# The sine product of q in rotary attention: from TensorE and VectorE to GpSimd

## What is computed

```python
def apply_rope(x, cos, sin):
    # rotate-half rotary on the last axis, x [B,T,H,2,64]
    x1, x2 = jnp.split(xf, 2, -1)
    return jnp.concatenate([x1 * cos - x2 * sin, x2 * cos + x1 * sin], -1)

def diff_attention(x, cos, sin, w_in, ...):
    q, k, v = jnp.split(x @ w_in, 3, axis=-1)
    q = apply_rope(q, cos, sin)
    k = apply_rope(k, cos, sin)
    lam = exp(sum(lam_q1 * lam_k1)) - exp(sum(lam_q2 * lam_k2)) + lambda_init
    ...
    s = einsum('bqhcd,bkhcd->bhcqk', q_blk, k) * scale     # causal
    p = softmax(s)
    p = p[:, :, 0] - lam * p[:, :, 1]
    o = einsum('bhqk,bkhe->bqhe', p, v)
    ...
    return (rms_norm(o, subln_w) * (1.0 - lambda_init)) @ w_out
```

## Time and profile before

| | us |
|---|---|
| median of 3 runs | 1422.12 |
| lowest and highest run | 1420.06, 1423.38 |
| the profiled execution, its own time | 1420.63 |
| span of that execution, first to last instruction | 1418.9 |

### The profile page before, as it was taken

One profiled execution on the slowest core, in us unless ns is written; L12 is line 12 of the kernel. 1 busy time (PEld: TensorE's weight loads), 2 busy tenths in 40 slices (PEclk: granted clock), 3 DMA queues, 4 the chain that ended last, 5 costly groups with the idle time before them and its releaser, 6 DMA issues.

```text
span 1418.9 us, 20021 instructions
## 1 busy us (share of the span) xinstructions
PE 1383.6 (98%) x7038; PEld 1135.0 (80%) x7038; DVE 869.4 (61%) x1362; ACT 635.3 (45%) x1033; POOL 80.8 (6%) x91
## 2 busy tenths in 40 slices
PE   8799999999999999999999999999999999999997
PEld 7688888888788888888888776667788888888886
DVE  4576677777586666666425537777686666664226
ACT  5666556666224444443212235666424444443211
POOL 3000000000000000000002011111000000000002
PEclk9999999999999999999999999999999999999999
DMA  6222111211222333334332222121223333334231
GB/s 195 55 65 68 45 51 52 63 55 60 75 60 67 100 100 89 103 96 152 105 104 74 89 60 60 45 74 59 90 60 89 89 103 92 100 118 134 89 104 60
DMA packets 157728, 118.85 MB, mean 84 GB/s; under 512 B 5899, under 2 KB 145645, under 8 KB 157677
## 3 DMA queue, kind: packets, MB, share of 16 engines
q1 hardware_dynamic: 157676, 118.17, 27.7%
HBM read 116.04 MB, written 2.11 MB: 83 GB/s over the span
## 4 chain that ended last, share of the span: by engine, by line
PE 90%; DVE 5%; ACT 3%; DMA 1%; issue 1%; SPq 0%; DVEq 0%; ACTq 0%
PE bank L1666 13%; PE bank L1668 13%; PE bank L1667 13%; PE bank L1681 10%; PE bank L1654 8%; PE bank L1655 8%; PE bank L1656 8%; PE bank L1735 3%; PE bank L2062 1%; PE bank L1742 1%; PE bank L2080 1%; PE bank L1733 1%; PE bank L2023 1%; PE bank L1751 1%; PE bank L1632 1%
## 5 line engine op out<-in xcount | busy, mean ns | idle before, releaser
L368 DVE TENSOR_TENSOR w_lo<-raw,w_hi 128x1024 fp32r<-128x1024 f32 x194 | 237.7, 1227 | 241.9 <-ACT w_hi L363 236.6
L1666 PE MATMUL bank<-x_hi,w_hi 128*128 128x512 f32 (+1 forms) x912 | 348.6, 382 | 2.6 <-DVE x_lo L1042 2.0
L1668 PE MATMUL bank<-x_hi,w_lo 128*128 128x512 f32 (+1 forms) x912 | 340.5, 373 | 0.0
L1667 PE MATMUL bank<-x_lo,w_hi 128*128 128x512 f32 (+1 forms) x912 | 340.2, 373 | 0.0
L363 ACT ACTIVATE w_hi<-raw 128x1024 fp32r<-128x1024 f32 x186 | 195.1, 1051 | 166.6 <-PE bank L1656 139.5
L1666 PEld LDWEIGHTS bank<-x_hi,w_hi 128*128 128x128 f32 x912 | 172.2, 189 | 33.8 <-DVE x_lo L1042 2.4
L1667 PEld LDWEIGHTS bank<-x_lo,w_hi 128*128 128x128 f32 x912 | 172.3, 189 | 30.2 <-issue 1.9
L1668 PEld LDWEIGHTS bank<-x_hi,w_lo 128*128 128x128 f32 x912 | 172.0, 189 | 30.4
L1654 PE MATMUL bank<-w_hi,u_hi 128*128 128x512 f32 x416 | 164.2, 395 | 0.6 <-DVE w_lo L368 0.6
L1656 PE MATMUL bank<-w_hi,u_lo 128*128 128x512 f32 x416 | 162.0, 389 | 0.0
L1655 PE MATMUL bank<-w_lo,u_hi 128*128 128x512 f32 x416 | 161.9, 389 | 0.0
(11 more groups left out here) (294 smaller groups left out, 2000.2 us busy)
## 6 DMA issues: line engine op xcount, KB each, us to landing
raw<-in_ffn_w_up SPq DMA_DIRECT2D x88, 512.0 KB, 3.8
raw<-in_ffn_w_down SPq DMA_DIRECT2D x44, 512.0 KB, 3.3
raw<-in_gdn_w_in SPq DMA_DIRECT2D x32, 512.0 KB, 4.1
raw<-in_diff_w_in SPq DMA_DIRECT2D x24, 512.0 KB, 3.8
raw<-in_gdn_w_out SPq DMA_DIRECT2D x8, 512.0 KB, 3.3
raw<-in_diff_w_out SPq DMA_DIRECT2D x8, 512.0 KB, 3.3
x_tok<-in_x SPq DMA_DIRECT2D x4, 512.0 KB, 5.9
ROW<-decay_rows SPq DMA_DIRECT2D x8, 256.0 KB, 4.6
```

The lines of the kernel that those rows point to most:

```text
L368: nc.vector.tensor_tensor(w_lo[:, s, :], raw[:, (base + r) % RAW, :], w_hi[:, s, :].bitcast(F32), ALU.subtract).then_inc(lo_ready, 1)
L1666: nc.tensor.matmul(out, hi, x_hi[:, k, cols], start=(k == 0), stop=False)
L1667: nc.tensor.matmul(out, hi, x_lo[:, k, cols], start=False, stop=False)
L1668: ins = nc.tensor.matmul(out, lo, x_hi[:, k, cols], start=False, stop=last)
```

## The change

The sine product of q no longer uses PE. After `rope_cos` of q, POOL makes `rope2` of q in four operations of 32 partitions: the inputs are 32 partitions of `qk_raw` and of `sin`, the output is the neighbouring 32 partitions of `rope2`, so the exchange of the halves is made by the output's place. POOL waits for each before the next. The sign is not in the product: DVE computes once, while the FFN of the layer before runs, a column of plus and minus ones from `swap` (`signs`), and its sum for `qr` becomes one operation, `rope2 * sign + rope1`. k keeps its matrix product. In the program of DVE the step of q moves behind `att_o`.

```diff
@@ -603,16 +604,27 @@
                 nc.gpsimd.tensor_tensor(rope1[kind][:, :], qk_raw[kind][:, :], cos[:, :],
                                         ALU.mult).then_inc(rope_pool, 1)

+            def rope_sin(g):
+
+                pool.wait_ge(rope_pool, 2 * g + 1)
+                for b in range(4):
+                    src, dst = slice(32 * (b ^ 1), 32 * (b ^ 1) + 32), slice(32 * b, 32 * b + 32)
+                    nc.gpsimd.tensor_tensor(rope2[0][dst, :], qk_raw[0][src, :], sin[src, :],
+                                            ALU.mult).then_inc(q_sin, 1)
+                    pool.wait_ge(q_sin, 4 * g + b + 1)
+
             def take_v(g):

                 nc.gpsimd.tensor_copy(vh[:, :, :], v_tok[:, :, ds(g * P, P)]).then_inc(v_head, 1)

             rope_cos(0, 0)
+            rope_sin(0)
             rope_cos(0, 1)
             take_v(0)
             with pool.Fori(0, HEADS - 1) as h:
-                for kind in range(2):
-                    rope_cos(h + 1, kind)
+                rope_cos(h + 1, 0)
+                rope_sin(h + 1)
+                rope_cos(h + 1, 1)
                 pool.wait_ge(t_pe, 1 + TP_N * h + TP["pv"])
                 take_v(h + 1)
             affine(3)
...
@@ -948,7 +960,7 @@

                 act.wait_ge(chunk_done, C_QK + 2 * g + kind + 1)
                 if not (isinstance(g, int) and g == 0):
-                    act.wait_ge(rope_pool, 2 * g + kind - 1)
+                    act.wait_ge(*((q_sin, 4 * g) if kind == 0 else (rope_pool, 2 * g)))
                 nc.scalar.activation(qk_raw[kind][:, :], bank[kind][:, :], ACT.Copy,
                                      scale=(HD ** -0.5 if kind == 0 else 1.0)).then_inc(bank_read[kind], 1)

...
@@ -1426,6 +1438,10 @@
                 dve.wait_ge(lam_dve, 1)
                 nc.vector.tensor_reduce(small[:, 0:2], lamp[:, :, :], AX.X, ALU.add).then_inc(lam_dve, 1)

+            def signs():
+
+                nc.vector.tensor_reduce(small[:, 7:8], swap[:, :], AX.X, ALU.add, negate=True).then_inc(sign_ready, 1)
+
             def lambda_rest():
                 dve.wait_ge(lam_act, 1)
                 nc.vector.tensor_tensor(small[:, 6:7], small[:, 3:4], small[:, 2:3], ALU.subtract).then_inc(lam_dve, 1)
...
@@ -1507,16 +1524,21 @@
             split_lo(dve, C_QK, 0, 2)
             dve.wait_ge(rope_act, 2)
             dve.wait_ge(lam_dve, LAM_DVE)
+            dve.wait_ge(sign_ready, 1)

             def rope(g, kind):
                 name = "qk"[kind]
                 last = R_DVE0 + RD_N * g
-                dve.wait_ge(rot_pe, 2 * g + kind + 1)
-                nc.vector.tensor_tensor(rope2[kind][:, :], bank[4 + kind][:, :], sin[:, :], ALU.mult).then_inc(rope_head, 1)
-                dve.wait_ge(rope_head, last + RD["rope2 " + name])
-                dve.wait_ge(rope_pool, 2 * g + kind + 1)
-                dst = (qr, kr)[kind]
-                nc.vector.tensor_tensor(dst[:, :], rope1[kind][:, :], rope2[kind][:, :], ALU.add).then_inc(rope_head, 1)
+                if kind == 0:
+                    dve.wait_ge(q_sin, 4 * g + 4)
+                    nc.vector.scalar_tensor_tensor(qr[:, :], rope2[0][:, :], small[:, 7:8], rope1[0][:, :], ALU.mult,
+                                                   ALU.add).then_inc(rope_head, 1)
+                else:
+                    dve.wait_ge(rot_pe, g + 1)
+                    nc.vector.tensor_tensor(rope2[1][:, :], bank[5][:, :], sin[:, :], ALU.mult).then_inc(rope_head, 1)
+                    dve.wait_ge(rope_head, last + RD["rope2 k"])
+                    dve.wait_ge(rope_pool, 2 * g + 2)
+                    nc.vector.tensor_tensor(kr[:, :], rope1[1][:, :], rope2[1][:, :], ALU.add).then_inc(rope_head, 1)

             def n_own(h, name):
                 dve.wait_ge(n_dve, ND_N * h + ND[name])
...
@@ -1594,12 +1616,13 @@
                 mix(3)
                 if more:
                     split_lo(dve, C_QK, it, 2 * r + 5)
-                    rope(h + 1, 0)
                 else:
                     hold_lo(dve, C_ATT_OUT + 5)
                 dve.wait_ge(t_pe, 1 + h * TP_N + TP["pv"])
                 nc.vector.tensor_scalar(att_o[:, :], bank[3][:, :], ROOT_MAX, -ROOT_MAX, ALU.min,
                                         ALU.max).then_inc(n_dve, 1)
+                if more:
+                    rope(h + 1, 0)
                 if not more:
                     hold_lo(dve, C_ATT_OUT + 6)
                 dve.wait_ge(n_act, NA_N * h + NA["sq"])
...
@@ -2017,10 +2040,10 @@
                         pe.wait_ge(bank_read[kind], T_QK // 2 + g + 1)
                     block_products(kind, (C_QK + 2 * odd + kind) % WS, k, k == KT - 1)

-            def rotate(g, kind):
-
-                wait_read(pe, kind, T_QK // 2 + g)
-                nc.tensor.matmul(bank[4 + kind][:, :], swap[:, :], qk_raw[kind][:, :], start=True,
+            def rotate_k(g):
+
+                wait_read(pe, 1, T_QK // 2 + g)
+                nc.tensor.matmul(bank[5][:, :], swap[:, :], qk_raw[1][:, :], start=True,
                                  stop=True).then_inc(rot_pe, 1)

             def turned_out(h):
...
@@ -2107,8 +2130,6 @@
                 turn(2)
                 fill(11, 13)
                 values(2)
-                if not last:
-                    rotate(h + 1, 0)
                 turn(3)
                 fill(13, 15)
                 values(3)
...
@@ -2118,7 +2139,6 @@
             pe.wait_ge(v_out, 2)
             project_qk(0, 0, 0, 2 * KT)
             pe.wait_ge(v_out, 2 * NT)
-            rotate(0, 0)
             step(0, 0)
             with pe.Fori(0, PAIRS - 1) as it:
                 for r in (1, 2):
```

More of the change, by code:

```diff
@@ L315, in build @@
         t_pe, t_dve, t_act, v_head = sem("t_pe"), sem("t_dve"), sem("t_act"), sem("v_head")
+        q_sin, sign_ready = sem("q_sin"), sem("sign_ready")
         rot_pe, rope_pool, rope_head = sem("rot_pe"), sem("rope_pool"), sem("rope_head")
@@ L1449, in down @@
                         lambda_rest()
+                        signs()
                 if l == 0:
@@ L2086, in step @@
                 fill(0, 1)
-                rotate(h, 1)
+                rotate_k(h)
                 fill(1, 3)
@@ L2158 @@
                      ("turn", 1), ("sc", 3, 0), ("sc", 3, 1), ("turn", 2), ("turn", 3), "pv"])
-RD, RD_N = numbered(["rope2 q", "qr", "rope2 k", "kr"])
+RD, RD_N = numbered(["qr", "rope2 k", "kr"])
 ND, ND_N = numbered(["oc", "ms", "inv", "flag", "o", "lo"])
```

## The result

| | before | with the change |
|---|---|---|
| median, us | 1421.24 (6 runs) | 1426.18 (6 runs) |
| lowest and highest, us | 1420.06, 1423.38 | 1425.38, 1428.22 |
| profiled execution, its own time and span, us | 1420.63, 1418.9 | 1425.85, 1424.1 |
| mean granted clock | 0.995 | 0.993 |

The ratio is 1.0037 with a 95% interval of 1.0024 to 1.0050: the change makes the kernel some 5 us slower, which is more than 0.2%. First the page of the changed kernel: busy time by engine, then the shares of the chain that ended last.

The account below looks back on a forecast made before the run. The tensor engine (PE), busy 98% of the span with 90% of the chain, was taken as the bound. 1.9 - 0.1 + 6 x 0.35 = +3.9 us on a median of 1422.12 gave 1426.0 us, range 1416 to 1432.

Parts of the forecast that it names:

- the sum of the change: Whole kernel: 1.9 us lost at the start, 0.1 gained to head 1, six steady heads 0.35 longer each: +3.9 us.
- Duration of a pass: Each GpSimd product of 32 partitions by 512 takes 1.27 us, since time goes by elements of a partition.
- The exclusion: GpSimd operations and VectorE operations with two SBUF inputs shut each other out for their whole length.
- some 0.13 us: In a collision, the held operation ends its own time less some 0.13 us after the one holding it.
- The walk through a steady head: Step-by-step times for head 3: held passes delay qr and kr, scores start at 929.95 instead of 929.62, 0.35 us longer.
- The start: Before head 0 nothing covers the passes; first scores at 845.0 instead of 843.08, 1.9 us lost.
- Then qr to 841.35: At the start, qr follows the last pass (840.61) and ends at 841.35, before POOL's cosine of k ends at 842.50.
- my third rival: Steady heads: GpSimd's cosine of k beats qr at 926.9; 0.9 us more in six heads, about 1431; chance 0.12.
- Head 0 to head 1: In this step pass 4 ends ahead of the reduction, 0.76 of 0.86 us is lost at Pm: gains 0.1 us.
- the rival of the clock: Longer PE waits at heads' ends bring the clock down in two to six heads: 3 to 9 us more; chance 0.12.
- The saving arrives: Pass 4 ends by 925.4, each of seven heads gives 0.86 us, distance 20.4: -6.0 us, about 1416; chance 0.20.
- half of it: Passes near 1.1 us or fewer collisions: heads within 0.3 us of today, start +1, 1420 to 1424; chance 0.12.

Follow-up runs that it names:

- the start repaired: The changed kernel, but q of head 0 made as before with swap product and VectorE product, passes only from head 1: 1423.68 us, ratio 1.0015.
- two passes: The changed kernel with two GpSimd passes of 64 partitions instead of four of 32, the exchange of the halves left out: 1417.04 us, ratio 0.9973.
- the last experiment: The changed kernel with GpSimd's four passes waiting until Pm of the head's fourth block is written: 1440.97 us, ratio 1.0136.

## Why the prediction was right, and where it was off

**The time.** Forecast 1426.0 us, measured 1426.18; range and direction hold. Two small errors cancel in that closeness: the sum of the change was +3.9 us where the medians differ by 4.9, and I started from a median of 1422.12 that six runs put at 1421.24. The mechanism and the sign were worked out; that the figure is only 0.2 us off is luck.

**Duration of a pass: 1.27 us, independent of the partitions.** Right: 1.26 to 1.30 alone for 32 partitions, 1.29 for the one free pass of 64, and 1.26 to 1.30 for the free cosine products of 128. The Trainium skill, GPSIMD Engine Reference, section 3.1, gives about 2.6 cycles an element, an estimate of 1.11 us; the trace disagrees by 0.16 us, and the measurement decides. By the page's figure a head would have been about 0.4 us shorter, about even with the kernel before, and the sign of the result less clear.

**The exclusion.** Right, and shown three ways: passes that nobody reads cost 3.6 us, the same DVE operation takes 1.66 us with its second input in SBUF and 0.68 with it in PSUM, and a single-input copy on POOL held kr. That is the rule of the Trainium skill, SBUF, State Buffer, section Who interferes with whom, and every row here agrees with it. The scaling of Eb (one input), which I let hold pass 1 by that rule, did: pass 1 took 1.42 us, not 1.27. One size was off: the "some 0.13 us" that a held operation gains fits passes, w_lo and kr, but a held Pm of 0.62 us ended 0.41 after its holder by the prediction's own rows, 0.21 less, and the fourth Pm of the changed kernel 0.19 less. It is worth 0.07 us.

**The walk through a steady head.** Shift it by 3.97 us, the later end of the cosine product, and compare: pass 1 ends 925.51 by the walk and 925.50 in the trace, Pm 926.13 and 926.06, pass 2 927.28 and 927.20, w_lo 928.36 and 928.28, pass 3 929.51 and 929.41, pass 4 930.85 and 930.78, kr 933.87 and 933.81, the scores 933.92 and 933.86. The net of +0.35 us a head (929.95 - 929.62 is 0.33) was measured as 0.30. What is late next was kr, as said, and two of its parts were tested alone: the copy of v is worth 0.25 us, and the swap product put back costs nothing.

**The start: +1.9 forecast, +2.4 measured.** The passes ended where they should (840.86 by the walk shifted by 0.25 us, 840.92 in the trace). The step that failed is "Then qr to 841.35": POOL's cosine product of k won the race by 0.05 us and held qr to 842.80. This is the mechanism of my third rival, which I had placed in the steady heads and not here. w_lo then was held by the copy of v. Together 0.5 us.

**Head 0 to head 1: -0.1 forecast, +0.7 measured.** The step that failed is the rival of the clock: I asked whether new waits inside the heads bring the clock down, and not whether the longer wait that I forecast at the start makes the old drop last longer. It did, 6.8 us at half clock instead of 3.4, and with the start repaired the step is 1.2 us shorter. Without it the passes gain 0.48 us there, more than the 0.1 that I walked: the walk kept the cosine product ahead of the third Pm, as in the earlier trace rows, and in the trace the race fell the other way, so that PE's wait of 0.96 us for that Pm is gone.

**The other rivals.** The clock did not fall within the heads of the change after waits of 1.35 us; that it falls after 2.4 us, at 1.55 us a time, one experiment shows. The change sat 1 us of wait a head away from a loss four times as large. The saving arrives when the passes are off POOL: 20.44 us a head, the very figure that I had named for it, and with two passes half of it.

## What to carry to other kernels

Before work is moved to an idle GpSimd, count its operations, not its elements, and look at what VectorE does beside them: each operation with two SBUF inputs there is shut out for a whole GpSimd operation. A VectorE operand left in PSUM avoided the conflict here. An operation of 32 partitions cost as much as one of 128, and the cost of a chain of them is not linear: here two fitted into a cushion of half a microsecond ahead of a late chain, and four did not.

When a saving lies on a busy engine, ask first whether that engine waits further on in the same period; here PE's product, put back, filled waits and cost nothing. And a wait that grows has a second price, the granted clock behind it, that can exceed the wait itself: 1.55 against 0.7 us a head in the last experiment.

## What the runs showed of the hardware that I had not expected

- Races between the two engines are decided by 0.03 to 0.13 us, and identical code falls differently in two places of one run: at the start POOL led by 0.05 us, in the steady heads DVE by 0.12.
- The clock after a wait of PE, in the profiled executions: no drop after 0.56, 1.35, 1.42, 1.74 and 1.79 us, a drop of some 3.4 us after 2.12, 2.15 and 3.56 us, of 6.8 to 6.9 us after 4.54, 5.12, 5.13 and 5.14. Between 2.3 and 2.5 us both occur: 2.31 and 2.38 without, 2.40 to 2.48 with. A drop of 3.4 us costs 1.0 to 1.6 us.
- The clock is not the same in all executions of one kernel: of the ten of the kernel with VectorE passes from SBUF, four have a mean clock of 0.996 and take 1415.9 to 1417.4 us, three have 0.994 and take 1418.8 to 1419.1. Differences of 2 us between medians can be the clock's.
- A single input in SBUF on VectorE is enough to hold a GpSimd pass (Eb, 1.42 against 1.27 us) and to be held by one (with the passes alone, Eb of the fourth block in head 0 takes 1.32 instead of 0.55 us). The reduction of the squares kept its 0.68 to 0.69 us beside GpSimd in all kernels, and the operations that read PSUM (the product of k, att_o) neither held GpSimd nor were held.
- Operations of 32 partitions whose output lies on other partitions than their inputs take the time of ordinary ones on both engines (1.27 us on POOL, 0.68 us on DVE).
